# Output projection of a hybrid decoder layer: tiles 0 and 1 share the pass over the groups of weights

## The chip, the cores and the metric

The kernel runs on one core of a Trainium2 chip. The metric is the device time of one execution in microseconds (us); lower is better. TensorE does the matrix products, ScalarE (ACT in the profile) and VectorE (DVE) the elementwise work, GpSimd (POOL) and SyncE (SP) issue the transfers between the device's memory and the on-chip buffers.

## The reference

The layer takes x of 2048 tokens by 1024 features in float32. A combined projection feeds three mixers (an S5 state space model, a Mamba-2 SSD and an mLSTM), whose outputs are concatenated, projected, normalised and added to x; then comes a SwiGLU channel mixer.

```python
mix = jnp.concatenate([y_a, y_b, y_c], axis=-1).astype(x.dtype) @ w_out   # 2048x2048 @ 2048x1024
x = x + rmsnorm(mix, norm_post_mix)
h = rmsnorm(x, norm_pre_ffn)
ff = (jax.nn.silu(h @ w_gate) * (h @ w_up)) @ w_down
return x + rmsnorm(ff, norm_post_ffn)
```

## The kernel before

The kernel is a row of phases, each a block of programs for the five engines, with a barrier of all engines between one phase and the next. The change lies in one of them, `phase_out`, which takes the concatenated mixer output y, finishes y @ w_out, applies the first norm and residual, and prepares the input of the channel mixer.

The 2048 tokens are 16 tiles of 128 (TT = 16). Each tile's y, of 2048 features, stands in memory split in an upper and a lower part (`y_hi`, `y_lo`), each 128 partitions by KM = 16 blocks by 128 tokens. A product in high precision is three matmuls: y_hi by w_hi, y_lo by w_hi, y_hi by w_lo, each 128x128 by 128x512.

The columns 0 to 511 of the result were mostly accumulated in the phase before and stand in memory as `first`; only KM-blocks 0 to 3 of them are added here. The columns 512 to 1023 are computed whole here. So the weights come in five groups of four blocks (WG = 4, GROUPS = 5): groups 0 to 3 are the 16 blocks for the right half, group 4 the four blocks for the left half. All five stay resident as `w_hi` and `w_lo`. A tile is 20 blocks by 3 = 60 matmuls, and a group of one tile is 12.

The order of the work is written out by hand, one program for each engine:

- SP loads group g of the weights into one of two raw buffers (`load_w`, L1699; from group 2 on it waits until the buffer's last use, `wlo_ok`, is past), and y of tile n into one of two pairs of buffers (`load_y`, L1705; from tile 2 on it waits for `mm_ok` of tile n - 2, since that tile's matmuls read the same buffer). All stand in one queue, in program order.
- ACT makes `w_hi` of each group (L1764, L1766; in groups 1 and 2 block by block, scaled by a gain), DVE makes `w_lo` (L1833, L1835) and signals `wlo_ok`.
- TensorE (`products`, `transposes`) works through tile 0's groups as `wlo_ok` allows; from then on the weights are there. After the products of tile n come the transposes of tile n - 1.
- After a tile's products (`mm_ok`): DVE adds `first` (L1843), ACT squares both halves (L1776, L1778), DVE and ACT make the norm's factor, DVE scales both halves (L1848, L1849; `read_ok` says that the tile's PSUM banks are read), adds the residual (L1853), ACT squares again (L1783), DVE scales into `xn` (L1859, `xn_ok`). TensorE transposes `xn` (L1885, `tr_ok`), ACT scales the result into the next phase's layout (L1798, `scaled`, `ht_ok`).
- POOL loads x and `first` of each tile and stores the results (L1725 to L1745).

There are two pairs of PSUM banks for products, so `products(n)` waits for `read_ok` of tile n - 2, and one pair for transposes, so `transposes(n)` waits for `ht_ok` of tile n - 1 as well as for `xn_ok` of its own. ACT's program after the weights is this loop, and the diff does not touch it:

```python
for n in range(TT):
    statistics(n)
    scaled(n)
```

Here `statistics(n)` is L1776 to L1783 of tile n with the two factors, and `scaled(n)` is L1798, which first waits for `tr_ok` of tile n.

Of the kernel before, what the change touches and what calls it, by code (L numbers as in the profile page):

```python
# [24 lines left out]
TT = T // P  # L25
# [1205 lines left out]
KM = DMIX // P  # L1231
WG, WM = 4, 2
# [428 lines left out]
def phase_out(nc, x, w_out, norm_gain, gain_mix, gain_ffn, ident, yhi_dram, ylo_dram, first_dram, x1_dram, hq_dram):  # L1661
# [3 lines left out]
    with ExitStack() as ctx:  # L1665
        sb, ps, sem = scope(nc, ctx)
        GROUPS = KM // WG + 1
        w_raw = sb("o_w_raw", [P, 2, WG, NB])
        w_hi, w_lo = sb("o_w_hi", [P, GROUPS * WG, NB], F32R), sb("o_w_lo", [P, GROUPS * WG, NB], F32R)
        y_hi, y_lo = sb("o_y_hi", [P, 2, KM, P], F32R), sb("o_y_lo", [P, 2, KM, P], F32R)  # L1670
# [6 lines left out]
        banks, tr_banks = ps("o_banks", [P, 2, 2, NB]), ps("o_tr", [P, 2, NB])  # L1677
        norm_col, norm_in = sb("o_norm", [P, GK]), sem("o_norm_in")
        const_in, w_in = sem("o_const_in"), (sem("o_w_in0"), sem("o_w_in1"))
        y_in, x_in = (sem("o_y_in0"), sem("o_y_in1")), (sem("o_x_in0"), sem("o_x_in1"))  # L1680
        x1_sent, h_sent = (sem("o_x1_sent0"), sem("o_x1_sent1")), [sem("o_h_sent%d" % r) for r in range(2 * QT)]
        t_ok, t_sent = sem("o_t_ok"), sem("o_t_sent")
        whi_ok, wlo_ok, act_chain, dve_chain = (sem("o_" + s) for s in ("whi_ok", "wlo_ok", "act_chain", "dve_chain"))
        mm_ok, sum_ok, ssq_ok, mean_ok, rstd_ok, read_ok, x1_ok, ssq2_ok, mean2_ok, rstd2_ok, xn_ok, tr_ok, ht_ok = (
            sem("o_" + s) for s in ("mm_ok", "sum_ok", "ssq_ok", "mean_ok", "rstd_ok", "read_ok", "x1_ok", "ssq2_ok",
                                    "mean2_ok", "rstd2_ok", "xn_ok", "tr_ok", "ht_ok"))
# [6 lines left out]
        @block.sync  # L1693
        def _(sp):
            def load_w(g):
                if g >= 2:
                    sp.wait_ge(wlo_ok, g - 1)
                src = w_tiles[:, WG * g:WG * (g + 1), NB:D] if g < GROUPS - 1 else w_tiles[:, 0:WG, 0:NB]
                sp.dma_start(w_raw[:, g % 2], src).then_inc(w_in[g % 2], 16)  # L1699

            def load_y(n):
                if n >= 2:
                    sp.wait_ge(mm_ok, n - 1)
                for dst, src in ((y_hi, yhi_dram), (y_lo, ylo_dram)):
                    sp.dma_start(dst[:, n % 2].bitcast(F32), src[n]).then_inc(y_in[n % 2], 16)  # L1705

            load_w(0)
            load_y(0)
            sp.dma_start(norm_col[:], norm_gain).then_inc(norm_in, 16)
            load_w(1)  # L1710
            for dst, src in ((gain_row[:], gain_mix.partition_broadcast(P)), (gain_col[:], gain_ffn), (ident_sb[:], ident)):
                sp.dma_start(dst, src).then_inc(const_in, 16)
            load_w(2)
            load_w(3)
            load_w(4)
            for n in range(1, TT):
                load_y(n)

        @block.gpsimd
# [143 lines left out]

        @block.tensor
        def _(pe):
            def products(n):
                b = n % 2
                pe.wait_ge(y_in[b], 32 * (n // 2 + 1))
                if n >= 2:
                    pe.wait_ge(read_ok, n - 1)  # L1870
                for k in range(KM + WG):
                    if n == 0:
                        pe.wait_ge(wlo_ok, k // WG + 1)
                    half, ky = (1, k) if k < KM else (0, k - KM)
                    for j, (y, w) in enumerate(((y_hi, w_hi), (y_lo, w_hi), (y_hi, w_lo))):
                        last = nc.tensor.matmul(banks[:, b, half, :], y[:, b, ky, :], w[:, k, :],  # L1876
                                                start=ky == 0 and j == 0, stop=k in (KM - 1, KM + WG - 1) and j == 2)
                last.then_inc(mm_ok, 1)

            def transposes(n):  # L1880
                pe.wait_ge(xn_ok, n + 1)
                if n >= 1:
                    pe.wait_ge(ht_ok, n)
                for k in range(KD):
                    last = nc.tensor.transpose(tr_banks[:, k // 4, k % 4 * P:(k % 4 + 1) * P],  # L1885
                                               xn[:, n % 2, k * P:(k + 1) * P], ident_sb[:])
                last.then_inc(tr_ok, 1)

            products(0)
            pe.wait_ge(const_in, 48)  # L1890
            for n in range(1, TT):
                products(n)
                transposes(n - 1)
            transposes(TT - 1)
# [682 lines left out]
```

## Time and profile before

| what | value |
|---|---|
| median of 3 runs | 3093.32 us (3090.63 to 3095.04) |
| the profiled execution's own time | 3091.88 us |
| its span | 3090.1 us |
| mean granted clock of TensorE | 0.968 of full speed |
| TensorE busy | 2885.1 us, 93% of the span |
| VectorE, ScalarE, GpSimd busy | 62%, 39%, 13% of the span |
| stretch of `phase_out` | from its first load at 1518.01 us to the next phase's first load at 1809.97 us |

The profile is one execution. The phases stand one after another in it, so that a shift of a phase's end is a shift of all that follows. A granted clock of 1.00 is 2.4 GHz, one of 0.50 is 1.2 GHz. Times of rows count from the span's start.

### The profile page before, as it was taken

The numbers are of one execution on the slowest core, as the hardware profiler recorded it, in microseconds if no ns is written. First come the engines' busy times: TensorE is split into PE (matmuls) and PEld (weight loads), VectorE is DVE, ScalarE is ACT, GpSimd is POOL, SyncE is SP. The second block draws the span as 40 slices with busy tenths as digits, with TensorE's granted clock in tenths as the row PEclk, the third lists the DMA queues.
The fourth block names the chain that finished last, engine by engine and source line by source line (L and its number), as shares of the span: only waits on it lengthen the run. The fifth ranks groups of instructions, "written<-read, shape, count | busy, mean of one in ns | idle before, by whom it ended". The sixth has DMA issues, their size and how long they took to land. (4 is left out here: it accounts for less than half of the span.)

```text
span 3090.1 us, 36088 instructions
## 1 busy us (share of the span) xinstructions
PE 2885.1 (93%) x13608; PEld 2324.3 (75%) x13608; DVE 1910.2 (62%) x2608; ACT 1196.3 (39%) x1996; POOL 389.4 (13%) x495
## 2 busy tenths in 40 slices
PE   7999999789999957999699949999999999999998
PEld 4788887577777636777578838888888888888887
DVE  4677887565643218888334357666676666565756
ACT  5322222453434324455233343333443333454543
POOL 0000000013430026566012100000000000000100
PEclk9999999899999978999899979999999999999999
DMA  4222333336665556877477764444543222676863
GB/s 148 65 67 89 127 128 103 121 132 208 208 200 157 154 180 225 277 263 265 185 260 287 257 214 157 159 158 157 181 174 130 107 107 104 256 255 193 294 194 112
DMA packets 295290, 545.15 MB, mean 176 GB/s; under 512 B 59308, under 2 KB 150860, under 8 KB 286284
## 3 DMA queue, kind: packets, MB, share of 16 engines
q1 hardware_dynamic: 263356, 437.69, 42.2%
q0 software_dynamic: 24704, 75.52, 6.8%
q10 hardware_dynamic: 7056, 29.63, 2.4%
q8 instruction: 108, 1.77, 0.2%
q14 instruction: 66, 0.54, 0.1%
HBM read 358.30 MB, written 184.44 MB: 176 GB/s over the span
## 5 line engine op out<-in xcount | busy, mean ns | idle before, releaser
L2406 PE MATMUL f_banks<-f_bop,f_w_op 128*128 128x512 f32 x3696 | 841.3, 390 | 31.5 <-DVE f_w_op L2233 29.7
L2406 PEld LDWEIGHTS f_banks<-f_bop,f_w_op 128*128 128x128 f32 x3696 | 695.4, 188 | 177.4 <-DVE f_w_op L2233 30.1
L2414 PE MATMUL f_banks<-f_d_op 128*128 128x512 f32 x1848 | 419.0, 389 | 0.0
L2414 PEld LDWEIGHTS f_banks<-f_d_op 128*128 128x128 f32 x1848 | 346.8, 188 | 72.0
L2297 DVE TENSOR_TENSOR f_d_op<-f_d_raw,f_d_op 128x1024 fp32r<-128x1024 f32 x154 | 187.6, 1225 | 148.8 <-ACT f_d_op L2150 148.1
L1146 PE MATMUL t_banks<-t_w_hi,h_hi 128*128 128x512 f32 (+1 forms) x640 | 248.3, 388 | 22.1 <-DVE t_w_lo L1018 22.1
L640 PE MATMUL c_banks<-h_hi,c_w_hi 128*128 128x512 f32 x640 | 255.7, 400 | 0.0
L640 PE MATMUL c_banks<-h_hi,c_w_lo 128*128 128x512 f32 x640 | 249.9, 390 | 0.0
L640 PE MATMUL c_banks<-h_lo,c_w_hi 128*128 128x512 f32 x640 | 249.1, 389 | 0.0
L2150 ACT ACTIVATE f_d_op<-f_d_raw 128x1024 fp32r<-128x1024 f32 x154 | 162.9, 1061 | 198.3 <-PE f_banks L2414 163.7
L1146 PE MATMUL t_banks<-t_w_hi,h_lo 128*128 128x512 f32 (+1 forms) x640 | 239.0, 373 | 0.0
L1146 PE MATMUL t_banks<-t_w_lo,h_hi 128*128 128x512 f32 (+1 forms) x640 | 238.8, 373 | 0.0
L2132 ACT ACTIVATE f_snap<-f_banks 128x1024 f32<-128x1024 f32 x88 | 90.3, 1026 | 259.9 <-PE f_banks L2406 259.9
L903 POOL DMA_DIRECT2D tokmaj<-t_out x96 | 52.8, 552 | 938.3 <-ACT t_out L941 938.3
L1146 PEld LDWEIGHTS t_banks<-t_w_hi,h_hi 128*128 128x128 f32 x640 | 122.6, 192 | 53.6 <-DVE t_w_lo L1018 23.4
L2233 DVE TENSOR_TENSOR f_w_op<-f_w_sum,f_w_op 128x1024 fp32r<-128x1024 f32 x66 | 80.9, 1225 | 129.1 <-ACT f_w_op L2120 128.3
L1876 PE MATMUL o_banks<-o_w_hi,o_y_hi 128*128 128x512 f32 x320 | 128.9, 403 | 25.0 <-DMA o_y_lo<-y_lo 16.2
L419 DVE SCALAR_TENSOR_TENSOR c_arena<-c_row,c_cw,c_arena 128x512 f32<-128x512 f32 x192 | 144.4, 752 | 6.8
L1018 DVE TENSOR_TENSOR t_w_lo<-t_raw,t_w_hi 128x1024 fp32r<-128x1024 f32 x72 | 87.1, 1224 | 92.9 <-ACT t_w_hi L934 92.1
L1146 PEld LDWEIGHTS t_banks<-t_w_hi,h_lo 128*128 128x128 f32 x640 | 122.8, 192 | 23.5 <-issue 3.8
L2233 DVE TENSOR_TENSOR f_w_op<-f_raw,f_w_op 128x1024 fp32r<-128x1024 f32 x88 | 107.8, 1225 | 52.1 <-ACT f_w_op L2120 49.9
L640 PEld LDWEIGHTS c_banks<-h_hi,c_w_lo 128*128 128x128 f32 x640 | 120.1, 188 | 26.1
(348 smaller groups left out, 4603.8 us busy)
## 6 DMA issues: line engine op xcount, KB each, us to landing
f_raw<-in_w_gu SPq DMA_DIRECT2D x88, 512.0 KB, 6.6
sop<-f_a SPq DMA_DIRECT2D x154, 256.0 KB, 2.0
f_d_raw<-sop SPq DMA_DIRECT2D x154, 256.0 KB, 2.8
t_raw<-in_w_tok SPq DMA_DIRECT2D x72, 512.0 KB, 4.2
f_d_raw<-top SPq DMA_DIRECT2D x88, 256.0 KB, 3.7
m_bc<-rows SPq DMA_DIRECT2D x16, 1152.0 KB, 6.8
f_d_raw<-in_w_dn SPq DMA_DIRECT2D x66, 256.0 KB, 3.0
o_y_hi<-y_hi SPq DMA_DIRECT2D x16, 1024.0 KB, 5.2
```

The costliest lines, as they stand in the source:

```text
L419: ins = nc.vector.scalar_tensor_tensor(conv[:, s], row[:, s, k:NB + k], cw[:, m, k:k + 1], conv[:, s], ALU.mult, ALU.add)
L640: last = nc.tensor.matmul(banks[:, p % RING, :], w[:, n % 2, k, :], h[:, k, q * NB:(q + 1) * NB], start=k == 0 and j == 0, stop=k == KD - ...
L903: pool.dma_start(tokmaj_dram[tile * P:(tile + 1) * P, to:to + width], out[:, e % 2, first:first + width]).then_inc(out_sent[e % 2], 16)
L1018: tt(w_lo[:, unit % 2, cols], raw[:, cols], w_hi[:, unit % 2, cols].bitcast(F32), sub).then_inc(wlo_ok, 1)
L1146: last = nc.tensor.matmul(banks[:, t, 0:width], h[:, k_first + k, tok], w[:, unit % 2, cols], start=begins and k == 0 and j == 0, stop=end ...
L1876: last = nc.tensor.matmul(banks[:, b, half, :], y[:, b, ky, :], w[:, k, :], start=ky == 0 and j == 0, stop=k in (KM - 1, KM + WG - 1) and ...
L2132: nc.scalar.activation(snap[:, slot], bank, ACT.Copy).then_inc(snap_ok, 1)
L2150: nc.scalar.activation(d_op[:, d % D_RING, 0:2], d_raw[:, d % S_RING], ACT.Copy).then_inc(dhi_ok, 1)
L2233: tt(w_op[:, t % W_RING, 1], src, w_op[:, t % W_RING, 0].bitcast(F32), sub).then_inc(wlo_ok, 1)
L2297: tt(d_op[:, d % D_RING, 2:4], d_raw[:, d % S_RING], d_op[:, d % D_RING, 0:2].bitcast(F32), sub).then_inc(dlo_ok, 1)
L2406: last = nc.tensor.matmul(bank[:, g, :], w_op[:, t % W_RING, w, cols], bop[:, s, h, k, :], start=begins and k == 0 and j == 0, stop=k == 3 ...
L2414: last = nc.tensor.matmul(banks[:, bank, :], d_op[:, d % D_RING, s, tok], d_op[:, d % D_RING, w, :], start=k == 0 and j == 0, stop=k == FU ...
```

## The change

TensorE gets a routine for tiles 0 and 1 together: group by group, the 12 matmuls of tile 0 and then the 12 of tile 1. The products of tile 2 follow, then the transposes of tiles 0 and 1, then the loop from tile 3 on. SP loads y of tile 1 right after y of tile 0, ahead of the norm gain and of the second group of weights. ACT, DVE and POOL keep their programs.

```diff
@@ SP
             load_w(0)
             load_y(0)
+            load_y(1)
             sp.dma_start(norm_col[:], norm_gain).then_inc(norm_in, 16)
             load_w(1)
...
             load_w(4)
-            for n in range(1, TT):
+            for n in range(2, TT):
                 load_y(n)
@@ TensorE
+            def row(n, k):
+                b = n % 2
+                half, ky = (1, k) if k < KM else (0, k - KM)
+                for j, (y, w) in enumerate(((y_hi, w_hi), (y_lo, w_hi), (y_hi, w_lo))):
+                    last = nc.tensor.matmul(banks[:, b, half, :], y[:, b, ky, :], w[:, k, :],
+                                            start=ky == 0 and j == 0, stop=k in (KM - 1, KM + WG - 1) and j == 2)
+                return last
+
+            def first_pair():
+                for g in range(GROUPS):
+                    pe.wait_ge(wlo_ok, g + 1)
+                    for n in range(2):
+                        if g == 0:
+                            pe.wait_ge(y_in[n], 32)
+                        for k in range(WG * g, WG * (g + 1)):
+                            last = row(n, k)
+                        if g == GROUPS - 1:
+                            last.then_inc(mm_ok, 1)
+
             def products(n):
-                b = n % 2
-                pe.wait_ge(y_in[b], 32 * (n // 2 + 1))
-                if n >= 2:
-                    pe.wait_ge(read_ok, n - 1)
+                pe.wait_ge(y_in[n % 2], 32 * (n // 2 + 1))
+                pe.wait_ge(read_ok, n - 1)
                 for k in range(KM + WG):
-                    if n == 0:
-                        pe.wait_ge(wlo_ok, k // WG + 1)
...
+                    last = row(n, k)
                 last.then_inc(mm_ok, 1)
...
-            products(0)
+            first_pair()
             pe.wait_ge(const_in, 48)
-            for n in range(1, TT):
+            products(2)
+            transposes(0)
+            transposes(1)
+            for n in range(3, TT):
                 products(n)
                 transposes(n - 1)
             transposes(TT - 1)
```

Three places show how instructions stand. The names in brackets are those under which the semaphores were first used in the program: in this phase `c_hraw_ok` is `xn_ok`, `c_hlo_ok` is `ht_ok`, `c_hhi_ok` is `tr_ok`, `c_k_mm` is `mm_ok`, `c_kern_sent` is `read_ok`, `c_x_in0` and `c_x_in1` are `y_in` of even and odd tiles.

The first is TensorE before, where tile 1's products end, tile 0's transposes stand, and tile 2's products begin:

```order
L1876 MATMUL o_banks<-o_w_hi,o_y_lo 128x512
L1876 MATMUL o_banks<-o_w_lo,o_y_hi 128x512
L1885 MATMUL o_tr<-o_ident,o_xn 128x128 [waits c_hraw_ok]
L1885 MATMUL o_tr<-o_ident,o_xn 128x128 x7
L1876 MATMUL o_banks<-o_w_hi,o_y_hi 128x512 [waits c_kern_sent,c_x_in0]
L1876 MATMUL o_banks<-o_w_hi,o_y_lo 128x512
L1876 MATMUL o_banks<-o_w_lo,o_y_hi 128x512
```

The same engine now, where tile 2's products end and tile 3's begin (L1898 is the transposes' new line, L1871 that of the products):

```order
L1871 MATMUL o_banks<-o_w_hi,o_y_lo 128x512
L1871 MATMUL o_banks<-o_w_lo,o_y_hi 128x512
L1898 MATMUL o_tr<-o_ident,o_xn 128x128 [waits c_hraw_ok]
L1898 MATMUL o_tr<-o_ident,o_xn 128x128 x7
L1898 MATMUL o_tr<-o_ident,o_xn 128x128 [waits c_hlo_ok,c_hraw_ok]
L1898 MATMUL o_tr<-o_ident,o_xn 128x128 x7
L1871 MATMUL o_banks<-o_w_hi,o_y_hi 128x512 [waits c_kern_sent,c_x_in1]
L1871 MATMUL o_banks<-o_w_hi,o_y_lo 128x512
L1871 MATMUL o_banks<-o_w_lo,o_y_hi 128x512
```

Tile 0's eight transposes moved from ahead of tile 2's products to behind them, and tile 1's eight follow them directly, with no products between the two.

The second place is ACT, between tile 0's first factor and tile 1's statistics, whose order is the same in both kernels:

```order
L1783 ACTIVATE o_junk,o_stat<-o_x 128x1024 [waits c_tab_sent]
L1770 ACTIVATE o_stat<-o_stat 128x1 [waits c_ones_mm,c_sq_ok]
L1771 ACTIVATE o_stat<-o_stat 128x1 [waits c_wt_ok]
L1798 ACTIVATE o_early<-o_tr,o_gain_col 128x128 [waits c_hhi_ok]
L1798 ACTIVATE o_early<-o_tr,o_gain_col 128x128 x7
L1776 ACTIVATE o_junk,o_stat<-o_banks 128x512 [waits c_k_mm]
L1778 ACTIVATE o_junk,o_stat<-o_work 128x512 [waits c_kern_ok,c_wt_ok]
```

Nothing moved here: tile 1's statistics (L1776 on) stand behind the eight activations that read tile 0's transposes.

The third is SP's queue at the start of the phase, as a piece of the difference:

```order
 L1705 DMA o_y_hi<-y_hi 128x2048
 L1705 DMA o_y_lo<-y_lo 128x2048
-L1709 DMA o_norm<-in_norm_gain 128x6
+L1705 DMA o_y_hi<-y_hi 128x2048
+L1705 DMA o_y_lo<-y_lo 128x2048
+L1710 DMA o_norm<-in_norm_gain 128x6
 L1699 DMA o_w_raw<-in_w_out 128x4x512
-L1712 DMA o_gain_row<-in_gain_mix 128x1024
-L1712 DMA o_gain_col<-in_gain_ffn 128x8
```

Tile 1's two loads of y moved from behind the last group of weights to ahead of the norm gain and group 1.

## Rows read from the trace of the kernel before

**Rows 1.** The page: busy us, share of the span and instructions of each engine.

```profile
PE 2885.1 (93%) x13608; PEld 2324.3 (75%) x13608; DVE 1910.2 (62%) x2608; ACT 1196.3 (39%) x1996; POOL 389.4 (13%) x495
```

**Rows 2.** Waits of the stretch 1510 to 1810: total us, times, longest.

```profile
PE o_banks L1876 <- DMA o_y_lo<-y_lo: 16.2, 1, 16.2
...
PE o_tr L1885 <- DVE o_xn L1859: 10.3, 1, 10.3
```

**Rows 3.** Timeline of tile 0's groups: start us, us, engine, line, operation.

```profile
1530.01 0.80 PE L1876 MATMUL o_banks<-o_w_hi,o_y_hi 128*128 128x512 f32 x1 [16.15 <-DMA o_y_lo<-y_lo]
...
1534.72 2.56 ACT L1764 ACTIVATE o_w_hi<-o_w_raw,o_norm 128x512 fp32r<-128x512 f32 x4 [9.75 <-DMA o_w_raw<-in_w_out]
1534.79 0.40 PE L1876 MATMUL o_banks<-o_w_lo,o_y_hi 128*128 128x512 f32 x1
...
1540.10 0.80 PE L1876 MATMUL o_banks<-o_w_hi,o_y_hi 128*128 128x512 f32 x1 [4.91 <-DVE o_w_lo L1833]
...
1542.89 1.28 DVE L1833 SCALAR_TENSOR_TENSOR o_w_lo<-o_w_raw,o_w_hi 128x512 fp32r<-128x512 f32 x2
...
1545.17 0.39 PE L1876 MATMUL o_banks<-o_w_hi,o_y_hi 128*128 128x512 f32 x1
...
1549.46 0.50 PE L1876 MATMUL o_banks<-o_w_hi,o_y_hi 128*128 128x512 f32 x1 [1.40 <-DVE o_w_lo L1835]
...
1554.96 0.65 PE L1876 MATMUL o_banks<-o_w_hi,o_y_hi 128*128 128x512 f32 x1 [2.49 <-DVE o_w_lo L1835]
```

**Rows 4.** The page: issues of a y load: times, size of one, us to landing.

```profile
o_y_hi<-y_hi SPq DMA_DIRECT2D x16, 1024.0 KB, 5.2
```

**Rows 5.** Windows: us, busy (times) of PE, PEld, DVE, ACT, POOL, granted clock, DMA share, GB/s.

```profile
1520.00:1538.00 18.00, 5.18 (x12) 3.82 (x12) 2.98 (x3) 4.47 (x5) 2.01 (x4) 0.59 1.03 401
1535.00:1538.00 3.00, 0.19 (x1) 0.00 (x0) 0.69 (x2) 2.27 (x4) 0.00 (x0) 1.00 1.04 371
1538.00:1540.00 2.00, 0.00 (x0) 0.00 (x0) 2.00 (x4) 0.85 (x2) 0.00 (x0) 0.52 0.17 62
...
1787.40:1789.50 2.10, 1.97 (x8) 1.57 (x8) 2.00 (x4) 0.04 (x1) 0.00 (x0) 0.50 0.00 0
```

**Rows 6.** Timeline, tile 0's end to tile 1's transposes.

```profile
1559.60 0.32 SPq L1705 DMA_DIRECT2D o_y_hi<-y_hi  x1
1559.96 0.44 SPq L1705 DMA_DIRECT2D o_y_lo<-y_lo  x1
...
1563.06 0.75 DVE L1849 SCALAR_TENSOR_TENSOR o_work<-o_banks,o_stat,o_gain_row 128x512 f32<-128x512 f32 x1
...
1573.02 1.03 PE L1885 MATMUL o_tr<-o_ident,o_xn 128*128 128x128 f32 x8
1573.81 0.48 PE L1876 MATMUL o_banks<-o_w_hi,o_y_hi 128*128 128x512 f32 x1
...
1587.53 1.04 PE L1885 MATMUL o_tr<-o_ident,o_xn 128*128 128x128 f32 x8
```

**Rows 7.** Tile o_y_lo, window 1559 to 1561: the second load of tile 2 to landing.

```profile
DMA to landing us min/median/max: 7.2/7.2/7.2
```

**Rows 8.** Timeline of ACT and DVE behind tile 0's transposes.

```profile
1574.09 2.18 ACT L1798 ACTIVATE o_early<-o_tr,o_gain_col 128x128 f32<-128x128 f32 x8 [7.05 <-PE o_tr L1885]
1576.11 0.65 ACT L1776 ACTIVATE o_junk<-o_banks 128x512 bf16<-128x512 f32 x1
...
1583.57 0.75 DVE L1859 TENSOR_SCALAR o_xn<-o_x,o_stat 128x1024 f32<-128x1024 f32 x1 [0.64 <-ACT o_stat L1771]
```

**Rows 9.** Timeline of the phase's end: the last two sets of transposes and the hand-over.

```profile
1776.13 1.03 PE L1885 MATMUL o_tr<-o_ident,o_xn 128*128 128x128 f32 x8
...
1787.46 1.97 PE L1885 MATMUL o_tr<-o_ident,o_xn 128*128 128x128 f32 x8 [10.30 <-DVE o_xn L1859]
...
1800.46 1.16 POOL L1745 DMA_DIRECT2D hq<-o_tq  x1 [7.18 <-DVE o_tq L1826]
1809.97 0.80 SPq L1990 DMA_DIRECT2D f_h_raw<-hq  x2
```

More of the change, by code:

```diff
@@ L1865, in _ @@
         def _(pe):
+            def row(n, k):
[15 more added lines that the diff above has]
+                            last.then_inc(mm_ok, 1)
             def products(n):
-                b = n % 2
-                pe.wait_ge(y_in[b], 32 * (n // 2 + 1))
-                if n >= 2:
-                    pe.wait_ge(read_ok, n - 1)
+                pe.wait_ge(y_in[n % 2], 32 * (n // 2 + 1))
+                pe.wait_ge(read_ok, n - 1)
                 for k in range(KM + WG):
-                    if n == 0:
-                        pe.wait_ge(wlo_ok, k // WG + 1)
[L1874 to L1877, printed above, removed]
+                    last = row(n, k)
                 last.then_inc(mm_ok, 1)
```

## The prediction

> **What bounds the kernel now.** I read the page first: TensorE is busy for 93% of the span [rows 1], so a change pays by what TensorE does not wait. In the waits of this phase TensorE has two large ones, 16.2 us for the first y (the phase's start) and 10.3 us ahead of the last transposes [rows 2]. Between them the timeline shows what the change is about. Tile 0 starts at 1530.01, when y has landed, and then goes from group to group in steps: 1530.01, 1540.10, about 1545.2, 1549.46, 1554.96 [rows 3]. Ahead of three of these it stands idle for 4.91, 1.40 and 2.49 us, waiting for `w_lo` [rows 3].
>
> The second thing to see is the clock. The 12 matmuls of the group at 1540.10 take until 1545.17, 5.07 us [rows 3], while the 60 of tile 2 take 1573.81 to 1587.53, 0.229 us each, so 2.74 us for 12 [rows 6]. The windows say why: the granted clock holds at 1.00 from 1535 to 1538 with TensorE idle nearly throughout, and is 0.52 from 1538 to 1540 [rows 5]. A restart after a long idle stretch thus costs 5.07 - 2.74 = 2.3 us.
>
> The third is what stands behind a tile on ACT and DVE. Tile 1's products end at 1573.02, but its first square, L1776, starts only at 1576.11, behind the eight activations of `scaled(0)`, which start at 1574.09 after tile 0's transposes [rows 6, 8]. Tile 1's `xn` starts at 1583.57 [rows 8] and takes 0.75. From tile 0's transposes to the end of tile 1's `xn` that is 1584.32 - 1573.02 = 11.3 us. Now tile 2's products hide it. At the phase's end nothing does, and it is seen bare: transposes at 1776.13, the next at 1787.46, 11.33 later, after 10.30 idle [rows 9].
>
> **The change, part by part.**
>
> *y of tile 1 ahead of group 1.* Two loads of 1024 KB [rows 4], 2.1 MB, go in front of the norm gain, group 1, the gains and group 2. The transfer engines are full from 1520 to 1538, DMA share 1.03 at 401 GB/s [rows 5], so all of these come 2.1 / 0.401 = 5.2 us later. Group 1's weights reached ACT at 1534.72 and let TensorE start at 1540.10 [rows 3]; now about 1545.3. Behind SP's waits, group 3 is issued at `wlo_ok` of group 1 and group 4 at that of group 2, so they shift along: group 2 is ready at 1542.89 + 1.28 + 5.2 = 1549.4, group 3 at 1554.7, group 4 at 1560.2 [rows 3]. The bounds of the shift are 0 and 2.1 / 0.371 = 5.7 us, by the slowest of the full windows [rows 5]; I take 5.2.
>
> *The pair.* Tile 0's group 0 runs 1530.0 to about 1535.2 as now. y of tile 1 lands about where group 1 landed plus 2.6, at 1537.4, and its 12 matmuls end by 1543 at either clock, before group 1 is ready; they cost nothing. From 1545.3 the 24 matmuls of group 1 take 5.07 + 2.74, to 1553.1; then 5.49 a group, each group's weights being ready before: 1558.6, 1564.1, 1569.6. Tile 0 is done at 1566.9, tile 1 at 1569.6, against 1573.02 now [rows 6]: TensorE is 3.4 us ahead. This is the gain of the change.
>
> *y of tile 2.* Its loads wait for tile 0's end, since they overwrite tile 0's buffers; y of tile 3 and all later ones queue behind them. Now tile 0 ends 13.4 us ahead of tile 1. With the pair it ends 2.7 us ahead. The loads issued at 1559.60 and 1559.96, and the second landed 7.2 after its issue [rows 6, 7]: 7.6 us behind tile 0's end. In the pair the issue comes 0.2 after the end, at 1567.1, and y lands at 1574.7. `read_ok` is no later: 1563.06 + 0.75 - 1559.60 = 4.2 us after the tile's end [rows 6], so 1571.3. So `products(2)` starts at 1574.7 instead of 1573.81: the 3.4 us have become +0.9. TensorE idles 5.1 us before it, about as long as ahead of 1540.10, so it restarts at the low clock: +2.3 (0 if the clock holds).
>
> *The transposes.* Before, `products(2)` is followed by `transposes(1)` alone. Now `transposes(0)` comes first, and `transposes(1)` right behind it. It waits for tile 1's `xn`, and that for tile 1's statistics, which on ACT stand behind `scaled(0)`, which waits for `transposes(0)`. Tile 1's products having been done 20 us earlier is of no use. So the 11.33 us of the phase's end [rows 9] stand bare here once more, and all later products queue behind that wait on TensorE. This adds 11.33 + 0.79 (the transposes that stood ahead of tile 2, 1573.02 to 1573.81 [rows 6]) = 12.1 us between the end of `products(2)` and `products(3)`. That cover, the 13.7 us of a tile's products, is what the new order takes away.
>
> The Trainium skill, "Perfetto Trace Analysis", section "Tensor Engine Instruction (MATMUL, LD_WEIGHTS)", says that ACT, DVE and GpSimd are strict in order. Here the trace agrees: L1776 at 1576.11 came behind L1798, though its tile was done at 1573.02 [rows 6, 8]. If ACT could pass ahead, the sum would be that of the first rival.
>
> *The restart after it.* Ten idle microseconds lower the clock, as at the end of the phase, where the eight transposes take 1.97 us at a granted clock of 0.50 against 1.04 [rows 5, 6]: +0.9. Then tile 3's products rise to the full clock: +2.3 if they restart as at 1540.10, nothing if the transposes have already brought the clock back. No row shows matmuls right behind such transposes; I take 1.5, between the two and nearer to the row that there is. With the transposes' own part that is 0.9 + 1.5 = 2.4.
>
> The Trainium skill, "TensorE: Matmul & The Clock Gate", section "Part 4: PE-mode transpose", says that the full clock doesn't engage for transposes. By it the term would be 0.9 + 2.3 = 3.2 and the sum 0.8 more. No row here shows whether it holds.
>
> *The rest.* From `products(3)` on, order and waits are as before: a tile's products cover the 11.3 us chain again (13.7 against 11.3), y loads are a tile ahead. The phase ends with the last stores and the next phase's first load at 1809.97 [rows 9], behind a barrier, so the shift stays whole. Nothing later can absorb it.
>
> **Sum.** 0.9 + 2.3 + 12.1 + 2.4 = 17.7 us. Against the profiled execution, span 3090.1 and time 3091.88, that is 3109.6. The median is 1.4 us above that execution; I say 3110.
>
> **Rivals.**
> *No bare chain (not slower).* The place is `transposes(1)`. If it waited hardly at all, what is left is 0.9 + 2.3 + 0.8 = +4.0 us: 3096, within what can be told from no change, which is about 0.2% or 6.2 us. It decides from a wait below some 2.2 us of the 10.5. For it speaks that tile 1's banks are full long before; against it, ACT's order in both kernels and rows 8 and 9. 4%.
> *The pair keeps its gain.* y of tile 2 in time as well, and no bare chain: -3.4 us, 3088.5. It would need the loads to land in 2.7 us, against 7.6 in the rows. 1%. The most that the idea could ever give is all of tile 0's waits and low clock: 120 matmuls from 1530.0 would end at 1557.5, 15.5 us ahead of 1573.02.
> *The clock or y is kinder.* The clock holds through the 5.1 us, or y of tile 2 lands sooner, or the chain is shorter by some: +11 to +15, 3103 to 3106. 10%.
> *The weights come later still.* If the moved loads cost the pair its lead (done at 1573 and not 1569.6), all later terms stay: +21.1, 3113; with one more low stretch 3115. 10%.
> *The forecast,* +15 to +20: 75%.
>
> **How the numbers follow.** All but the first two cases are slower by over 0.2%: 95%; same 4%; faster 1%, since even the pair's whole gain is 0.11%. The range runs from 3104 (clock kind, y soon) to 3115 (no lead, rule of transposes); it leaves out the first two rivals and the ends of the next two.
>
> **What would show it.** In the profile after: `w_hi` of group 1 starts near 1539.9; tile 1's products end near 1569.6; a wait of `products(2)` for `o_y_lo` of about 5 us; a wait of about 10.3 us of the transposes for `o_xn`, beside the one at the phase's end; a granted clock near 0.5 behind both; periods of 14.5 us from tile 3 on. The prediction is wrong if the second `o_xn` wait is missing, or if the next phase's first load comes earlier than some 1816.

## The result and the profile after

The changed kernel takes 3108.89 us, the median of 4 runs (3103.30 to 3112.37), against 3093.90 us before (4 runs, 3090.63 to 3095.04). The ratio is 1.005 with a 95% interval of 1.0038 to 1.0063: slower by 15 us, and by 12 to 19 us if the interval is taken.

The profiled execution is the fastest of the four, at 3103.30 us, and its span is 3101.5 us, only 11.4 above that of before. So the phase has to be measured by itself. Its first load and the next phase's first load, in SP's timeline:

```profile
1515.58 0.38 SPq L1699 DMA_DIRECT2D o_w_raw<-in_w_out  x1
...
1823.43 0.80 SPq L2006 DMA_DIRECT2D f_h_raw<-hq  x2
```

The phase takes 307.85 us. It took 1809.97 - 1518.01 = 291.96 (the end is in [rows 9], the start in the table of the profile before): +15.9. The phases ahead of it were 2.4 us shorter in this execution, those behind 2.1; their code is the same in both kernels, so this is what executions differ by, not an effect of the change.

TensorE's busy time hardly moved (2885.1 before [rows 1]):

```profile
PE 2887.7 (93%) x13608; PEld 2326.7 (75%) x13608; DVE 1910.9 (62%) x2608; ACT 1195.4 (39%) x1996; POOL 389.4 (13%) x495
```

The waits of the phase, in total us, times and longest, answer to [rows 2]:

```profile
PE o_banks L1871 <- DMA o_y_lo<-y_lo: 23.4, 3, 16.2
...
PE o_tr L1898 <- DVE o_xn L1860: 20.6, 2, 10.3
```

The wait for y now has three parts: the phase's start, 1.93 us for tile 1 and 5.21 us for tile 2. The wait of the transposes for `xn` stands there twice at 10.3 us, where it stood once. The waits for `w_lo` between the groups, 8.8 us in three pieces before, have shrunk to one of 3.53. The timeline shows all of it in order, with ACT's start on group 1 and SP's issue of tile 2's y among TensorE's rows:

```profile
1527.67 0.77 PE L1871 MATMUL o_banks<-o_w_hi,o_y_hi 128*128 128x512 f32 x1 [16.25 <-DMA o_y_lo<-y_lo]
...
1534.55 0.50 PE L1871 MATMUL o_banks<-o_w_hi,o_y_hi 128*128 128x512 f32 x1 [1.93 <-DMA o_y_lo<-y_lo]
...
1537.30 2.56 ACT L1765 ACTIVATE o_w_hi<-o_w_raw,o_norm 128x512 fp32r<-128x512 f32 x4 [14.76 <-DMA o_w_raw<-in_w_out]
1542.68 0.80 PE L1871 MATMUL o_banks<-o_w_hi,o_y_hi 128*128 128x512 f32 x1 [3.53 <-DVE o_w_lo L1834]
...
1546.87 0.39 PE L1871 MATMUL o_banks<-o_w_hi,o_y_hi 128*128 128x512 f32 x1
...
1563.39 0.34 SPq L1705 DMA_DIRECT2D o_y_hi<-y_hi  x1
...
1571.29 0.77 PE L1871 MATMUL o_banks<-o_w_hi,o_y_hi 128*128 128x512 f32 x1 [5.21 <-DMA o_y_lo<-y_lo]
1587.36 1.03 PE L1898 MATMUL o_tr<-o_ident,o_xn 128*128 128x128 f32 x8
1598.70 1.97 PE L1898 MATMUL o_tr<-o_ident,o_xn 128*128 128x128 f32 x8 [10.30 <-DVE o_xn L1860]
1615.56 1.03 PE L1898 MATMUL o_tr<-o_ident,o_xn 128*128 128x128 f32 x8
```

And the windows, cut at these events (busy us and times of PE, PEld, DVE, ACT, POOL; granted clock; DMA share; GB/s):

```profile
1515.58:1566.08 50.50, 32.94 (x120) 25.89 (x120) 13.25 (x15) 13.78 (x18) 2.19 (x4) 0.77 0.64 240
1566.08:1571.29 5.21, 0.00 (x1) 0.03 (x1) 3.22 (x5) 1.55 (x4) 1.61 (x3) 0.82 1.01 423
1571.29:1587.36 16.07, 16.07 (x61) 12.99 (x61) 1.09 (x2) 0.00 (x0) 0.00 (x0) 0.85 0.46 177
1587.36:1598.70 11.34, 1.04 (x10) 0.80 (x8) 3.97 (x8) 5.43 (x18) 2.54 (x4) 0.76 0.75 279
1598.70:1615.56 16.86, 16.86 (x69) 14.04 (x70) 4.61 (x8) 5.44 (x18) 2.53 (x4) 0.86 0.49 156
```

The pair is done 50.5 us into the phase, where tile 1 was done at 55.0 (1573.02 - 1518.01 [rows 6]). Then come 5.21 us of nothing, tile 2's products with a stretch at the low clock (16.07 against 13.72 us), 11.34 us with 8 transposes in them, and a second slow restart (16.86 against the 14.5 of a normal period). ACT's window of 16.07 us in which it does nothing at all, 0.00 (x0), shows it standing at `scaled(0)` while tile 1's banks are full; what it does afterwards lies bare in the next window. The rows of ACT and DVE name what each waits for (L1799 is `scaled`, L1777 and L1779 are the two squares, L1844 adds `first`):

```profile
1571.73 0.69 DVE L1844 TENSOR_TENSOR o_work<-o_first,o_banks 128x512 f32<-128x512 f32 x1
1588.43 1.91 ACT L1799 ACTIVATE o_early<-o_tr,o_gain_col 128x128 f32<-128x128 f32 x7 [17.60 <-PE o_tr L1898]
1590.44 0.65 ACT L1777 ACTIVATE o_junk<-o_banks 128x512 bf16<-128x512 f32 x1
1592.04 0.16 DVE L1846 TENSOR_TENSOR o_stat<-o_stat 128x1 f32<-128x1 f32 x1 [19.62 <-ACT o_junk L1779]
```

DVE did its part for tile 1 at 1571.73 and then stood for 19.62 us until ACT's square; ACT stood for 17.60 us until tile 0's transposes, and took up tile 1 only behind them. So nothing that tile 1 itself still needed was late: it was ACT's order that held it.

### The profile page after: what moved, and what is told of

Read it like the earlier page. It is cut to its first block and busy times, and to the rows that moved or that the text cites. A ratio compares the mean times of both kernels' runs of the same rounds, so it can differ in the third digit from the quotient of the medians.

```text
span 3101.5 us, 36087 instructions
## 1 busy us (share of the span) xinstructions
PE 2887.7 (93%) x13608; PEld 2326.7 (75%) x13608; DVE 1910.9 (62%) x2608; ACT 1195.4 (39%) x1996; POOL 389.4 (13%) x495
## 5 line engine op out<-in xcount | busy, mean ns | idle before, releaser
L1871 PE MATMUL o_banks<-o_w_hi,o_y_hi 128*128 128x512 f32 x320 | 130.1, 407 | 26.9 <-DMA o_y_lo<-y_lo 23.4
```

## The experiments

The profiled execution's phase is given beside each time. It is one execution for each kernel, and stretches of the same code differ by some 2 us between executions, so a difference of 2 or 3 us between two phases carries weight only with the rows that explain it. All ratios are to the kernel before, on the same chip, with 95% intervals; its median is 3093.90 beside the change, 3092.3 beside the first four experiments and 3092.5 beside the last two.

| kernel | time us | ratio | interval | phase us |
|---|---|---|---|---|
| before | 3093.90 | | | 291.96 |
| the change | 3108.89 | 1.005 | 1.0038 to 1.0063 | 307.85 |
| tile 0's transposes first | 3097.10 | 1.0012 | 1.0002 to 1.0021 | 295.74 |
| only the load moved | 3096.09 | 1.0008 | 0.9999 to 1.0018 | 294.96 |
| only the transposes moved | 3106.92 | 1.0040 | 1.0026 to 1.0053 | 301.87 |
| tile 0 ahead in the pair | 3094.09 | 1.0004 | 0.9995 to 1.0013 | 292.39 |
| y of tile 2 in two parts | 3089.02 | 0.9988 | 0.9979 to 0.9997 | 286.21 |
| the same, y of tile 2 whole | 3091.76 | 0.9997 | 0.9988 to 1.0006 | 288.31 |

**Tile 0's transposes back ahead of tile 2's products**, the rest of the change kept:

```diff
-            products(2)
             transposes(0)
+            products(2)
             transposes(1)
```

> The changed kernel with tile 0's transposes back ahead of tile 2's products; all else of the change stays. Theory (the bare chain of tile 1's statistics carries most of the loss): the second 10.3 us wait for o_xn is gone, and with it the restart behind it; what stays is that tile 2's products begin 1.8 us later than before (xn of tile 0 is ready 0.4 us behind y of tile 2, and the transposes take 0.8 to 1.5) and restart at the low clock (up to 2.3): phase 295.5 to 296.1 us against 292.0 of before and 307.9 of the change, time about 3098. Rival (the loss comes from the moved loads or from the late y of tile 2): the time stays within 4 us of the change's, above 3104.

Measured: phase 1817.09 - 1521.35 = 295.74, ratio 1.0012. Twelve of the sixteen microseconds are gone by a change of one line's place. Its timeline, first load, the transposes and the end:

```profile
1521.35 0.38 SPq L1699 DMA_DIRECT2D o_w_raw<-in_w_out  x1
...
1577.87 1.94 PE L1898 MATMUL o_tr<-o_ident,o_xn 128*128 128x128 f32 x8 [5.77 <-DVE o_xn L1860]
1579.47 0.78 PE L1871 MATMUL o_banks<-o_w_hi,o_y_hi 128*128 128x512 f32 x1
...
1594.65 1.03 PE L1898 MATMUL o_tr<-o_ident,o_xn 128*128 128x128 f32 x8
...
1817.09 0.80 SPq L2006 DMA_DIRECT2D f_h_raw<-hq  x2
```

The wait of 5.77 is now for tile 0's `xn`, and none for y of tile 2 is left behind it. No wait stands ahead of the transposes at 1594.65. The theory's number was met, the rival's (above 3104) was not.

**Only the load moved**, in the kernel before:

```diff
             load_y(0)
+            load_y(1)
             sp.dma_start(norm_col[:], norm_gain).then_inc(norm_in, 16)
...
-            for n in range(1, TT):
+            for n in range(2, TT):
```

> The kernel before with y of tile 1 loaded ahead of the norm gain and of group 1, and nothing else of the change. Theory (the transfer engines are full there and TensorE waits for the weights): group 1 reaches ACT 5.0 us later, each later group too, tile 0 ends 5 us later and so does all that follows: phase 297.0 against 292.0 us, time about 3099. Rival (the weights wait for ACT, DVE and the raw buffers and not for the transfers): less than 1 us.

Measured: phase 1816.00 - 1521.04 = 294.96, 3.0 longer, not 5.0; the ratio's interval still touches 1. TensorE's timeline:

```profile
1521.04 0.38 SPq L1699 DMA_DIRECT2D o_w_raw<-in_w_out  x1
...
1548.21 0.79 PE L1877 MATMUL o_banks<-o_w_hi,o_y_hi 128*128 128x512 f32 x1 [9.93 <-DVE o_w_lo L1834]
...
1557.56 0.50 PE L1877 MATMUL o_banks<-o_w_hi,o_y_hi 128*128 128x512 f32 x1 [2.15 <-DVE o_w_lo L1836]
...
1562.57 0.50 PE L1877 MATMUL o_banks<-o_w_hi,o_y_hi 128*128 128x512 f32 x1 [0.41 <-DVE o_w_lo L1836]
1565.62 0.34 SPq L1705 DMA_DIRECT2D o_y_hi<-y_hi  x1
...
1816.00 0.80 SPq L1991 DMA_DIRECT2D f_h_raw<-hq  x2
```

Group 1 starts 27.2 us into the phase, against 22.1 [rows 3]: the 5 us are there, as a wait of 9.93 instead of 4.91. Group 4 starts at 41.5, against 36.95: 4.6. The rest went in group 4 itself, which took 3.05 us to the issue of tile 2's y and had taken 4.64 (1554.96 to 1559.60 [rows 3, 6]): its wait is 0.41 in place of 2.49, and its granted clock is 1.00. The low clock had come one group sooner, in group 3 behind the wait of 2.15 (the mean granted clock is 0.63 from 1557.56 to 1562.16), where it filled time in which TensorE would have waited for group 4's weights. So the theory's shift of the weights is right, and what it does to the end is smaller in this execution because the low stretch fell where it cost next to nothing.

**Only the transposes moved**, in the kernel before:

```diff
-            for n in range(1, TT):
+            products(1)
+            products(2)
+            transposes(0)
+            transposes(1)
+            for n in range(3, TT):
                 products(n)
                 transposes(n - 1)
```

> The kernel before with tile 0's transposes moved behind tile 2's products, and nothing else: no pair, no moved load. Theory (bare chain): products of tile 2 begin 0.8 us sooner, then 11.34 us from one set of transposes to the next with a 10.3 us wait for o_xn, then 16.9 us instead of 14.5 for the restart at the low clock: phase 292.0 + 12.9 = 304.9 us, time about 3107. Rival (the wait only shows up because tile 1's products end early in the pair, or it is covered here since tile 1's statistics start right behind its products): less than 4 us.

Measured: ratio 1.004 (8 to 16 us). The profiled execution is the lowest of its five, 3100.60; its phase is 1819.35 - 1517.48 = 301.87, 9.9 longer than before. The timeline:

```profile
1517.48 0.38 SPq L1699 DMA_DIRECT2D o_w_raw<-in_w_out  x1
...
1556.79 0.32 SPq L1705 DMA_DIRECT2D o_y_hi<-y_hi  x1
...
1583.81 1.03 PE L1885 MATMUL o_tr<-o_ident,o_xn 128*128 128x128 f32 x8
1595.15 1.97 PE L1885 MATMUL o_tr<-o_ident,o_xn 128*128 128x128 f32 x8 [10.31 <-DVE o_xn L1859]
...
1611.37 1.04 PE L1885 MATMUL o_tr<-o_ident,o_xn 128*128 128x128 f32 x8
...
1819.35 0.80 SPq L1994 DMA_DIRECT2D f_h_raw<-hq  x2
```

The wait of 10.31 us and the 11.34 between the two sets are those of the change, though there is no pair here and no moved load, and though tile 1's products end 13.6 us earlier than tile 2's. The second term, 16.22 us to the next transposes where 16.9 were expected, was 0.7 smaller. The rest of the gap to the expected 304.9 lies ahead of the edit, in code that is that of before: tile 0 is done 39.3 us into the phase where it was done at 41.6 (1559.60 - 1518.01 [rows 6]), because group 4 found the clock still high. The rival's bound of 4 us is passed by both measures.

**Tile 0 ahead in the pair**, on top of the first experiment: groups 0 to 2 alternate as in the change, then come tile 0's groups 3 and 4, then tile 1's.

```diff
-                for g in range(GROUPS):
+                for n, g in ((0, 0), (1, 0), (0, 1), (1, 1), (0, 2), (1, 2), (0, 3), (0, 4), (1, 3), (1, 4)):
...
```

> As the first of this set, and in the pair the last groups go in the order tile 0 group 3, tile 0 group 4, tile 1 group 3, tile 1 group 4. Theory (y of tile 2 can only be loaded once tile 0 is done, 7.9 us ahead of its use): tile 0 ends 4.3 us sooner, at 43.7 us of the phase in place of 48.0, y and xn land at 51.6 and 52.0 instead of 55.7 and 56.1, TensorE waits for them 1.5 us instead of 5.2 and the clock holds: phase about 289 us, time about 3091, 3 us below before. Rival (the gain of the pair is lost for another reason than tile 0's late end): the same as the first of this set, phase 295.5 to 296.1.

Measured: phase 1812.39 - 1520.00 = 292.39, ratio 1.0004. It is 3.3 us better than the first experiment in the profile and 3.0 in the medians, but not the 289 that was expected: it lies midway between that and the rival's 295.5.

```profile
1520.00 0.38 SPq L1699 DMA_DIRECT2D o_w_raw<-in_w_out  x1
...
1565.40 0.34 SPq L1705 DMA_DIRECT2D o_y_hi<-y_hi  x1
...
1573.85 1.40 PE L1897 MATMUL o_tr<-o_ident,o_xn 128*128 128x128 f32 x8 [3.04 <-DVE o_xn L1860]
1574.91 0.78 PE L1871 MATMUL o_banks<-o_w_hi,o_y_hi 128*128 128x512 f32 x1
...
1812.39 0.80 SPq L2005 DMA_DIRECT2D f_h_raw<-hq  x2
```

Tile 0 is done at 45.4 us of the phase, sooner than the change's 47.8 (1563.39 in its timeline) but not at 43.7: I had counted 4.3 us, but moving two groups ahead saves only the 12 matmuls of tile 1's group 3, 2.7 us. The wait stayed at 3.04 and the clock did fall, in the middle of the transposes. The direction and the size, 3.3 us for an end 2.7 us sooner, speak for the theory; the larger saving was an error in my arithmetic.

**Everything bound to tile 0's end taken out of the way.** On top of the last: y of tile 1 behind group 1 of the weights, tile 0's transposes after the first 12 matmuls of tile 2's products, and y of tile 2 in two parts, blocks 4 to 15 as soon as tile 0's group 3 has read them.

```diff
-            load_y(1)
             sp.dma_start(norm_col[:], norm_gain).then_inc(norm_in, 16)
             load_w(1)
+            load_y(1)
...
+            for free, at, blocks in ((early_ok, 1, slice(WG, KM)), (mm_ok, 1, slice(0, WG))):
+                sp.wait_ge(free, at)
+                for dst, src in ((y_hi, yhi_dram), (y_lo, ylo_dram)):
+                    sp.dma_start(dst[:, 0, blocks].bitcast(F32), src[2][:, blocks]).then_inc(y_in[0], 16)
...
+                    if (n, g) == (0, GROUPS - 2):
+                        last.then_inc(early_ok, 1)
...
                 for k in range(KM + WG):
+                    if n == 2 and k == WG:
+                        transposes(0)
                     last = row(n, k)
...
```

> The pair with tile 0 ahead in its last groups, y of tile 1 loaded behind group 1 of the weights, tile 0's transposes after the first 12 matmuls of tile 2's products, and y of tile 2 loaded in two parts: blocks 4 to 15 when tile 0's group 3 is done, blocks 0 to 3 when all of tile 0 is. Theory (the pair's lead is lost only by what is bound to tile 0's end, and by the weights behind y of tile 1): group 1 starts at 22.1 us of the phase as before, the pair ends near 49.1, y of tile 2 is in by then, no restart and no bare chain; products of tile 3 begin near 64.5 in place of 70.3: phase about 286.2 us against 292.0 of before, time about 3087. Rival (something else holds tile 2 back): phase 289 or more.

Its partner differs only in loading y of tile 2 whole:

> As the split load's kernel, but y of tile 2 loaded whole once tile 0 is done. Theory (the load of y behind tile 0's end is what is late next): tile 0 ends near 43.6 us of the phase, y is in at 51.4, TensorE waits some 2.3 us ahead of tile 2's products, and may restart at the low clock: phase 288.5 (clock holds) to 290.8 us, time 3090 to 3092. Rival (the load is hidden): the same as with the split load, 286.

Measured: phases 1802.86 - 1516.65 = 286.21 and 1805.77 - 1517.46 = 288.31, ratios 0.9988 (0.9979 to 0.9997) and 0.9997 (0.9988 to 1.0006). Both phases are where the theory had them, 286.2 and 288.5. The timed intervals of the two overlap, so it is the rows that tell them apart. TensorE with the split load:

```profile
1516.65 0.38 SPq L1699 DMA_DIRECT2D o_w_raw<-in_w_out  x1
...
1538.49 0.77 PE L1875 MATMUL o_banks<-o_w_hi,o_y_hi 128*128 128x512 f32 x1 [4.84 <-DMA o_y_lo<-y_lo]
1568.55 1.09 PE L1905 MATMUL o_tr<-o_ident,o_xn 128*128 128x128 f32 x8
...
1580.41 1.03 PE L1905 MATMUL o_tr<-o_ident,o_xn 128*128 128x128 f32 x8
...
1802.86 0.80 SPq L2012 DMA_DIRECT2D f_h_raw<-hq  x2
```

From 1538.49 on there is no wait in the pair, none ahead of tile 2 and none between the two sets of transposes, which are 11.86 us apart with 48 matmuls between them. With the load whole, one wait is back, and the trace names no releaser for it:

```profile
1517.46 0.38 SPq L1699 DMA_DIRECT2D o_w_raw<-in_w_out  x1
...
1568.73 0.47 PE L1871 MATMUL o_banks<-o_w_hi,o_y_hi 128*128 128x512 f32 x1 [2.26 <-issue]
...
1805.77 0.80 SPq L2006 DMA_DIRECT2D f_h_raw<-hq  x2
```

It is 2.26 us where 2.3 were expected, and the clock held through it. That it is y of tile 2 follows from the pair of kernels, which differ in nothing else, and the 2.1 us between their phases are about that wait. Between the fourth experiment and this one two things changed at once, where y of tile 1 is loaded and where tile 0's transposes stand, and their shares of the 4.1 us were not separated.

## Why the prediction was right

3110 was forecast, 3108.89 measured, and the sign and the mechanism were those of the sum. Step by step, in the profiled execution:

- **The weights come 5.2 us later.** Group 1 reached ACT 21.7 us into the phase against 16.7: 5.0. The load alone in the kernel before gave the same 5 us ahead of group 1, and 3.0 at the phase's end.
- **The pair is 3.4 us ahead.** It was 4.5 (50.5 against 55.0 us). The step that was off is the restart of group 1, taken at 2.3: its first 12 matmuls took 1542.68 to 1546.87, 4.19 us against 2.74, so 1.45. The idle stretch ahead of it was shorter than before, 3.5 us against 4.91, but that is not shown to be the reason: the same 12 matmuls took 4.32 us behind the 9.93 idle of the second experiment and 5.07 behind the 4.91 of before.
- **y of tile 2 turns the lead into +0.9.** It turned it into -0.1: tile 2 started 7.9 us behind the issue of its y (1563.39 to 1571.29), against 7.6 counted to the landing, and tile 0 had ended sooner by the step above. This is where the pair's gain went: with the transposes in order, the pair and its load are no better than the load alone (295.74 against 294.96). Ending tile 0 2.7 us sooner, which brings both its `xn` and y of tile 2 forward, shortened the phase by 3.3 us, and the split load alone, which brings only y forward, by 2.1, down to 286.21.
- **The restart of tile 2: +2.3.** 16.07 - 13.72 = 2.35.
- **The bare chain: +12.1.** The 11.33 us between the transposes are 11.34. But the 0.79 that I added for the moved set is wrong: 11.33 is counted from start to start and holds that set already. The term is 11.3. Moved alone, the transposes cost 8 to 16 us timed; taken back alone, they give back 12.1 us of the phase. That the wait is ACT's order is read from the rows of ACT and DVE above; no run changed that order.
- **The restart behind it: 2.4.** 16.86 - 14.51 = 2.35, against the normal period of 1587.53 - 1573.02 = 14.51 [rows 6]. That it comes so close is in part luck: the 1.5 in it was a choice between 0 and 2.3, and the same term was 16.22 - 14.51 = 1.7 in the third experiment. Here a rule of the Trainium skill was weighed, by which it would be 3.2 (last section).

With these, -0.1 + 2.35 + 11.34 + 2.35 = 15.9, which is the phase's growth; the medians are 15.0 apart. The 17.7 was too large by 1.0 in the first stretch and by the 0.8 counted twice. That the median lies within 1.1 us of the forecast is therefore luck as well: the four times spread over 9 us.

Of the rivals, the one without a bare chain described the first experiment: it gave +4.0, and taking the chain away left +3.8. The one in which the pair keeps its gain needed the load of y to fit into 2.7 us; making it fit by other means gives 5.8 us of the phase, and 3.5 us in the medians. Neither happened in the change itself, for the reasons given, ACT's order and tile 0's late end.

What remains open: the timed ratios are less sharp than the phases. The medians of the load alone, of tile 0 ahead in the pair and of y of tile 2 loaded whole can't be told from before. Why stretches of the same code differ by 2 us between executions is explained only for group 4 (last section).

## What to carry to other kernels

When work is moved on one engine, follow its consumer's queue, not only its data: the transposes were needed by ACT before it would look at tile 1, and 12 us hung on one line's place. Sharing weights between two tiles moves the first tile's end towards the second's, and all that is bound to that end (the reload of its buffer, the release of its banks) moves with it; let the first tile run ahead once its weights are there, and free its buffer in parts. A bare chain at a phase's end is a price list: it shows what any cover is worth before one takes it away.

## What the runs showed of the hardware

Whether a short wait costs a restart as well varies. Group 4 of tile 0 follows a wait of 2.49 us in before and runs eight matmuls and part of a ninth at the low clock (4.64 us for the group); with a wait of 1.74 in the third experiment, on the same code, it takes 3.05 us. In other runs the clock held through 2.26 us (with y of tile 2 loaded whole; the granted clock is 1.00 over the 12 matmuls behind it) and fell behind 3.04; behind 2.15 us in the second experiment two matmuls ran at the full clock before it fell. So the length of the wait alone does not decide it in these rows. For group 4, the shorter wait and the kept clock together make 2.3 us in when tile 0 is done, 41.6 against 39.3 us of the phase, in code that is the same.

How long a restart stays at the low clock varies too. In the eight profiles of this phase, where idle stretches of 2.49 to 16.5 us stand ahead of products with no transposes between, 6 to 11 matmuls run at the low clock before it rises. Both ends are found in one execution, that of the change. Behind 3.53 us of idle it rises in the seventh matmul, behind 5.21 us in the twelfth:

```profile
1545.41 0.47 PE L1871 MATMUL o_banks<-o_w_hi,o_y_hi 128*128 128x512 f32 x1
...
1576.12 0.47 PE L1871 MATMUL o_banks<-o_w_lo,o_y_hi 128*128 128x512 f32 x1
```

Behind eight transposes that are themselves at the low clock (1.62 us, granted 0.50, after some 6 to 10 us of idle) it is seven matmuls in the change and in the first experiment, which is within that spread, and three and most of a fourth in the third experiment, which is below it:

```profile
1598.20 0.58 PE L1876 MATMUL o_banks<-o_w_hi,o_y_hi 128*128 128x512 f32 x1
1598.62 0.39 PE L1876 MATMUL o_banks<-o_w_hi,o_y_lo 128*128 128x512 f32 x1
```

The first matmul of that run started at 1596.77. The Trainium skill, "TensorE: Matmul & The Clock Gate", section "Part 4: PE-mode transpose", says that the full clock does not engage for transposes. The third experiment speaks against it as a rule for what follows such transposes, the other two runs fit either way, and one run does not settle it. Transposes that follow products with no wait, as at 1587.36, do run at a granted clock of 1.00: eight in 1.03 us.
